# Loading each page of a paged latent cache in two transfers instead of one

## What is computed

```python
ckv_past   = cache_latent[l, page_table]   # 8 sequences x 32 pages x 128 rows x 256
krope_past = cache_k_rope[l, page_table]   # the same rows x 32
s_past = einsum('bqhc,bkc->bhqk', q_lat, ckv_past) + einsum('bqhr,bkr->bhqk', q_rope, krope_past)
p = softmax(concat([s_past, s_new]) * scale)
o = einsum('bhqk,bkc->bqhc', p[..., :P], ckv_past) + einsum('bhqk,bkc->bqhc', p[..., P:], ckv_new)
```

## Time and profile before

| | |
|---|---|
| median of 3 runs | 1517.12 us (1513.87 to 1520.32) |
| profiled execution: its own time | 1516.65 us |
| profiled execution: span, first to last instruction | 1514.7 us |
| mean granted TensorE clock | 0.963 of full speed |
| busy share of the span: PE, DVE, ACT, POOL | 92%, 41%, 28%, 25% |
| DMA: mean rate, busy share of 16 engines on the queue that SP feeds | 116 GB/s, 34.2% |
| the chain that ended last: PE, DVE, ACT, DMA, POOL, SP's issuing | 73%, 9%, 5%, 4%, 3%, 2% |

### The profile page before, as it was taken

One profiled execution on the slowest core, in us unless ns is written; L12 is line 12 of the kernel. 1 busy time (PEld: TensorE's weight loads), 2 busy tenths in 40 slices (PEclk: granted clock), 3 DMA queues, 4 the chain that ended last, 5 costly groups with the idle time before them and its releaser, 6 DMA issues.

```text
span 1514.7 us, 28473 instructions
## 1 busy us (share of the span) xinstructions
PE 1394.7 (92%) x11800; PEld 1275.6 (84%) x11800; DVE 614.1 (41%) x950; ACT 416.8 (28%) x672; POOL 371.8 (25%) x385
## 2 busy tenths in 40 slices
PE   6999999999989997988888789999999999999995
PEld 6999989999989974444445689999999999999994
DVE  5234335224354666333343553335532332322324
ACT  5232211221233200322232332223422222222223
POOL 3219253245221064422220000001221021021023
PEclk9999999999989986999999899999999999999997
DMA  5223212223232143699995112222222322322311
GB/s 214 78 64 112 76 63 89 90 63 95 60 93 88 42 140 118 231 316 319 325 334 218 42 59 94 86 84 84 84 76 75 99 77 76 98 85 68 100 46 66
DMA packets 72449, 175.22 MB, mean 116 GB/s; under 512 B 9505, under 2 KB 10434, under 8 KB 72290
## 3 DMA queue, kind: packets, MB, share of 16 engines
q1 hardware_dynamic: 70306, 169.69, 34.2%
q0 software_dynamic: 2048, 4.20, 0.9%
HBM read 170.85 MB, written 3.00 MB: 115 GB/s over the span
## 4 chain that ended last, share of the span: by engine, by line
PE 73%; DVE 9%; ACT 5%; DMA 4%; POOL 3%; SPq 2%; issue 2%; DVEq 0%; POOLq 0%; ACTq 0%
PE d L1304 63%; SPq L294 2%; DVE w_lo L847 2%; ACT w_hi L418 2%; DMA kv_w<-kv_src 2%; PE e L1470 1%; PE e L1493 1%; DVE x_lo L852 1%; PE d L1567 1%; DMA kv_hl<-kv_src 1%; DVE rstd L857 1%; PE d L1577 1%; PE e L1473 1%; POOL hid L680 1%; DMA kv_raw<-kv_src 1%
## 5 line engine op out<-in xcount | busy, mean ns | idle before, releaser
L847 DVE TENSOR_TENSOR w_lo<-raw,w_hi 128x1024 fp32r<-128x1024 f32 (+2 forms) x200 | 232.9, 1165 | 648.7 <-ACT w_hi L418 648.3
L1304 PE MATMUL d<-x_hi,w_hi 128*128 128x272 f32 x1824 | 383.6, 292 | 21.0 <-DVE w_lo L847 10.0
L1304 PE MATMUL d<-x_hi,w_lo 128*128 128x272 f32 x1824 | 380.5, 290 | 0.0
L1304 PE MATMUL d<-x_lo,w_hi 128*128 128x272 f32 x1824 | 379.2, 290 | 0.0
L418 ACT CAST w_hi<-raw 128x1024 fp32r<-128x1024 f32 (+2 forms) x200 | 191.5, 957 | 536.6 <-PE d L1304 536.6
L1304 PEld LDWEIGHTS d<-x_hi,w_hi 128*128 128x128 f32 x1824 | 289.9, 190 | 25.6 <-DVE x_lo L852 10.2
L1304 PEld LDWEIGHTS d<-x_lo,w_hi 128*128 128x128 f32 x1824 | 289.9, 191 | 0.0
L1304 PEld LDWEIGHTS d<-x_hi,w_lo 128*128 128x128 f32 x1824 | 287.7, 191 | 0.0
L680 POOL TENSOR_TENSOR hid<-silu,up 128x544 f32<-128x544 f32 x44 | 59.5, 1353 | 512.3 <-DVE up L875 512.0
L1304 PE MATMUL d<-hid_hi,w_hi 128*128 128x272 f32 x704 | 153.5, 301 | 24.0 <-POOL hid_lo L682 21.9
L1304 PE MATMUL d<-hid_hi,w_lo 128*128 128x272 f32 x704 | 150.9, 297 | 0.0
(11 more groups left out here) (304 smaller groups left out, 1568.6 us busy)
## 6 DMA issues: line engine op xcount, KB each, us to landing
raw<-w_gu SPq DMA_DIRECT2D x88, 512.0 KB, 3.4
kv_w<-kv_src SPq DMA_DIRECT2D x80, 256.0 KB
kv_raw<-kv_src SPq DMA_DIRECT2D x72, 256.0 KB
kv_hl<-kv_src SPq DMA_DIRECT2D x72, 256.0 KB
raw<-w_post SPq DMA_DIRECT2D x34, 512.0 KB, 3.5
raw<-w_d1b SPq DMA_DIRECT2D x16, 384.0 KB, 3.2
raw<-w_d2b SPq DMA_DIRECT2D x16, 384.0 KB, 3.3
raw<-w_in SPq DMA_DIRECT2D x10, 512.0 KB, 3.4
```

Of the source, the lines that this page charges most:

```text
L847: nc.vector.tensor_tensor(w_lo[:, s % 2, 0:n, :], raw[:, s % NRAW, 0:n, :], w_hi[:, s % 2, 0:n, :].bitcast(FP), ALU.subtract).then_inc(S.l ...
L1304: ins = mm(d[:, par, b, 0:HALF], w[:, pos, c0 + k, :], x[:, k, b * HALF:(b + 1) * HALF], start=first, stop=stop)
```

## The change

Each page is issued as two transfers into the same buffer: first the floats 0 to 255 of each of the 128 rows (the transposed half), then the floats 256 to 511. Both count the same semaphore up, so PE waits for twice the count. Bytes, buffers, the order of the units, and what PE waits for (all of the unit) stay.

```diff
             if v >= NKV:
                 sp.wait_ge(S.un_pv, v - NKV + 1)
             for g, page in enumerate(pages):
-                load(kv_of(v)[:, g, :], a["kv_src"][bass.ds(page, 1)].rearrange("a p n -> p (a n)"), sem["unit_in%d" % (v % NKV)])
+                for x in range(2):
+                    load(kv_of(v)[:, g, x * KV_LORA:(x + 1) * KV_LORA],
+                         a["kv_src"][bass.ds(page, 1), :, x * KV_LORA:(x + 1) * KV_LORA].rearrange("a p n -> p (a n)"),
+                         sem["unit_in%d" % (v % NKV)])
 
@@
         def unit_scores(v):
             b = v // UPB
-            pe.wait_ge(sem["unit_in%d" % (v % NKV)], 16 * UNIT * (v // NKV + 1))
+            pe.wait_ge(sem["unit_in%d" % (v % NKV)], 16 * 2 * UNIT * (v // NKV + 1))
             pe.wait_ge(sem["rope_in%d" % (v % NKR)], 16 * UJ * (v // NKR + 1))
```

## The result

The changed kernel takes 1575.3 us (median of 4 runs, 1573.9 to 1580.4) against 1518.7 us: 1.038 of before (95% interval 1.035 to 1.041), 57 us slower. Forecast were 1564, and 1538 to 1588 as the range. Its profiled execution took 1580.4 us, with a span of 1578.5.

A forecast was written before the change was run, and what follows sets the result against it. Page transfers were taken to bound the stage at 7.03 us a unit, SP's issuing after the change at 8.83. 1516.65 + 45.7 + 1 for the clock = 1563.4, plus 0.5 to the median: 1564, range 1538 to 1588.

The forecast's parts named there:

- The step that decides: SP's queue in the page stage: 8 added issues at 0.517 us make issuing the limit, 8.83 us a unit against 7.03.
- The loop through the buffers: PE's values, SP's next issues and their landing through three buffers: 16.2 us for two periods, 8.1 each, under 8.83.
- the length of a unit on SP: SP's queue: 16 issues of a unit take 15 x 0.517 + 0.33 = 8.09 us, 8.83 with the gap.
- back pressure of full queues: SP's queue: stretches of issues held up by full queues, 1.41 us in one unit, would be swallowed.
- The sum done the other way round: SP in the page stage: 103 us of added issues, about half swallowed by 48.8 us of waits and held-up issues, leaving some 46.
- the clock: PE in the page stage: standing lowers its clock, slower matmuls lie under SP's wait, 1 us added for the last unit.
- idle cover: SP's wait for free buffers, 48.8 us in 23 waits: 2.1 us a unit under which issues can be added.
- Hidden issues: SP's queue: issue time goes by bytes, transfers stay the limit at 7.03 us a unit, 1516.65 or a few us less; 8%.
- Dear issues of 0.62 us: SP's queue: every issue takes 0.43 us, a unit takes 10.5 us, time 1607; chance 3%.
- Choked transfers: Page transfers: half-size rows slow the DMA engines to 9.8 us a unit, 69 us longer, 1586; chance 7%.
- The cheap second issue: SP's queue: the second half's issue costs 0.39 us, a unit 7.81 us with the gap, 21 us later, 1538; chance 8%.

The follow-up runs named there:

- one-issue kernel: Kernel before, with each page still one transfer but of 256 rows of 1 KB, its row halves going to different buffer places: 1533.1 us, 1.012 of before.
- partition cut: Kernel before, with each page issued as two transfers of 64 rows of 2 KB instead of one of 128 rows: 1633.1 us, 1.076 of before.
- moved step: Kernel before, with the scores of unit v + 1 on PE put last in a step, after the turns and values: 1.006 of before.
- 12 issues: Kernel before, with 4 of 8 pages of a unit in two halves by columns and the other 4 whole: 1.015 of before.

## Why the prediction was right, and where its sizes were off

**The step that decides held.** Issue 333 ns whatever the bytes, distance 0.517 us, gap 0.74 (measured 0.73), SP without waits, unit 7 at 641.31 (said: 640.75), share 0.81 and 240 GB/s (said: 0.7 to 0.8 and about 250). The loop through the buffers, said to be the next-latest thing, kept off SP's path as well: in the changed kernel SP starts a unit at least 0.48 us after its buffer is free (units 7 to 28), where a waiting SP needs 0.20. The one-issue kernel, the partition cut and the moved step show that it is the issues and not the rows.

**A term was too small: the length of a unit on SP.** I took 8.09 us; the mean is 8.60, because about one issue in 28 lasts 0.6 to 1.8 us. With 0.75 for the gap that makes 9.35 instead of 8.83, and over the 24 steps to unit 31 the start moves from 854.75 to 868.28: 13 of the 17 us by which the profiled execution exceeds my 1563.4. Such issues stand in the rows of before, too (1232 ns in the earlier trace rows, units of 4.71 and 5.36 us in the earlier trace rows). I read them as the back pressure of full queues, which SP's issuing would end. They were there with a share of 0.81 as well: that reading was wrong. The sum done the other way round leaned on it too. 103 us less the 48.8 of waits are 55, and only by letting the stretched issues vanish did it come down to 46.

**The rest.** Unit 31 is scored 11.6 us after its first issue, I had 10.4: 1.2 us. From there to the end of the span are 698.7 us against 695.3, of which I gave 1 for the clock. The clock of the stage fell to 0.86 with PE's standing, and this lay under SP's pace as said: the end of the values comes 5.1 instead of 4.1 us after the scores of the next unit, and the period is SP's. For the same reason PE's waits for pages (those of its weight loads) rose by 37 us, from 29.4 to 66.0, and not by the 45 that were said. The profiled execution is itself 5 us above the median of its kernel, which brings 1580 back to 1575.

**A side argument was wrong.** I called the 48.8 us of SP's waits idle cover, 2.1 us a unit, and the transfers the limit of before. With 12 issues the loss begins while SP waits 40 us. Its waits are one part of a closed loop of 13.8 us. The cover was whole in the kernel with the moved step, where neither that loop nor the transfers are on the path. For 16 issues the sum did not depend on it: the wrong reading cost nothing because SP alone needs more than any other part.

**The rivals.** Hidden issues: refuted by the durations. Dear issues of 0.62 us: refuted by the median of 333 ns. Choked transfers: refuted by 282 GB/s with rows of 1 KB. By the Trainium skill (DMA: Bandwidth & Descriptors, "Why small descriptors are slow (HBM only)") such rows would cost the transfers 4.5% (an estimate from its figures), 8 us in the prediction's reckoning. The one-issue kernel lost 17 us, with 8 at the lower end of its interval; it also has dearer issues, so the estimate is neither confirmed nor refuted. The cheap second issue: refuted, since SP runs a register instruction and a move for each, and without them 0.47 us would be left.

## What to carry to other kernels

Count a DMA queue's issues as work with a rate: number of issues x distance between their starts, plus the gap between groups, against the period of the stage; the issuer is then one more engine that can bind. Its waits in the profile need not be a free reserve: ask first whether a loop through few buffers runs through the issuer, because then its waits are a part of the period. In the kernel with the moved step, where the loads were off the path, they were one. Take the mean length of a group of issues from the trace, not the shortest, since the rare long ones stay when the issuer becomes the bound.

## What was not expected of the hardware

The time of an issue goes with the shape of the transfer; bytes or rows alone do not order it: 333 ns for 128 rows of 2 KB or of 1 KB, 468 ns for 64 rows of 2 KB, 543 ns for 256 rows of 1 KB in two levels. Issues with nothing between them settle at 0.47 us apart, lasting 432 ns each instead of 333. The kernel with added rows of 16 B kept the DMA engines at a share of 0.91 for 235 GB/s, where the changed kernel, on another chip, has 0.81 for 240. Issues of 0.6 to 1.8 us turn up about every 17 to 19 us before and after the change, 19 of 22 beside a transfer of 16 KB on the instruction queue. And pages cut by partitions moved at 197 GB/s with a share of only 0.66 (window 660 to 810 us), as fast as SP issued them.
